# Convolution norm and swish in two pieces ahead of the recurrence's turns, block inverse by predicated copy on 128 partitions

## What is computed

```python
# conv group: GLU -> causal depthwise conv (width 31) -> LayerNorm over channels -> swish
mu = jnp.mean(of, axis=-1, keepdims=True)
var = jnp.mean(jnp.square(of - mu), axis=-1, keepdims=True)
of = (of - mu) * lax.rsqrt(var + LN_EPS) * ln_g + ln_b
conv_out = jax.nn.silu(of)
# rwkv group, per token and head
sa = jnp.einsum('bhvk,bhk->bhv', S, -kk_t)
S = S * w_t[:, :, None, :] + sa[..., None] * (kk_t * a_t)[:, :, None, :] + v_t[..., None] * k_t[:, :, None, :]
y = jnp.einsum('bhvk,bhk->bhv', S, r_t)
x = x + concat(conv_out, rwkv_out) @ w_out
```

## Time and profile before

| | us |
|---|---|
| median of 3 runs | 1161.65 |
| lowest and highest run | 1160.74, 1165.13 |
| span of the profiled execution (no other time of it is given) | 1161.0 |
| PE busy | 1105.8 (95%) |
| DVE busy | 671.7 (58%) |
| ACT busy | 364.6 (31%) |
| POOL busy | 216.2 (19%) |

### The profile page before, as it was taken

One profiled execution on the slowest core, in us unless ns is written; L12 is line 12 of the kernel. 1 busy time (PEld: TensorE's weight loads), 2 busy tenths in 40 slices (PEclk: granted clock), 3 DMA queues, 4 the chain that ended last, 5 costly groups with the idle time before them and its releaser, 6 DMA issues.

```text
span 1161.0 us, 24215 instructions
## 1 busy us (share of the span) xinstructions
PE 1105.8 (95%) x9392; PEld 668.9 (58%) x9393; DVE 671.7 (58%) x1144; ACT 364.6 (31%) x720; POOL 216.2 (19%) x278
## 2 busy tenths in 40 slices
PE   7999999999999799999999999967999999999987
PEld 5666666666666788999984555534333333333343
DVE  6388999993554788888744232365343443434416
ACT  6000011011322657777641211022223232222324
POOL 4000000010001213323320001002233342332200
PEclk9999999999998899999999999977999999999998
DMA  9211111010000111111242321057999899999739
GB/s 280 69 36 37 37 37 43 20 43 23 1 1 5 16 21 19 19 18 18 52 148 83 109 73 47 35 221 289 394 350 324 306 326 346 416 407 407 297 126 388
DMA packets 97151, 170.92 MB, mean 147 GB/s; under 512 B 44362, under 2 KB 68609, under 8 KB 87779
## 3 DMA queue, kind: packets, MB, share of 16 engines
q1 hardware_dynamic: 89571, 151.79, 36.8%
q0 software_dynamic: 7488, 17.84, 4.4%
HBM read 153.11 MB, written 25.91 MB: 154 GB/s over the span
## 4 chain that ended last, share of the span: by engine, by line
PE 82%; DVE 9%; DMA 5%; ACT 1%; issue 1%; SPq 1%; POOLq 0%; DVEq 0%; ACTq 0%
PE ps L1654 27%; PE ps L2119 14%; PE ps L1969 10%; PE ps L2149 7%; PE ps L1666 6%; PE ps L1687 3%; PE ps L2106 2%; DMA arena<-in_w_exp_up_dram 2%; PE ps L2184 2%; PE ps L1675 1%; DVE arena L2457 1%; PE ps L1999 1%; DMA arena<-in_w_exp_down_dram 1%; DVE arena L2460 1%; DVE arena L2423 1%
## 5 line engine op out<-in xcount | busy, mean ns | idle before, releaser
L1654 PE MATMUL ps<-arena 128*128 128x384 f32 (+1 forms) x1032 | 316.6, 468 | 0.0
L1654 PEld LDWEIGHTS ps<-arena 128*128 128x128 f32 x1032 | 195.3, 190 | 118.0 <-issue 1.9
L2119 PE MATMUL ps<-arena 128*64 x416 | 188.5, 596 | 3.5 <-DVE arena L2874 2.0
L2122 PE MATMUL ps<-arena 128*64 128x512 f32 x416 | 188.5, 596 | 0.0
L2271 DVE SCALAR_TENSOR_TENSOR arena<-arena,cw 128x1024 f32<-128x1024 f32 x240 | 168.2, 777 | 0.4
L2119 PEld LDWEIGHTS ps<-arena 128*64 128x64 f32 x416 | 54.4, 136 | 112.2 <-issue 112.1
L1969 PE MATMUL ps<-arena 128*128 128x512 f32 x256 | 113.1, 596 | 0.0
L1666 PE MATMUL ps<-arena 64*64 64x64 f32 x2960 | 98.2, 219 | 5.9 <-DVE arena L2471 1.7
L2149 PE MATMUL ps<-arena 128*64 x208 | 96.5, 607 | 2.4 <-ACT arena L1411 2.4
L1666 PEld LDWEIGHTS ps<-arena 64*64 64x64 f32 x2960 | 92.3, 135 | 8.6 <-issue 4.7
L2152 PE MATMUL ps<-arena 128*64 128x512 f32 x208 | 96.5, 607 | 0.0
(11 more groups left out here) (365 smaller groups left out, 1536.1 us busy)
## 6 DMA issues: line engine op xcount, KB each, us to landing
arena<-in_w_exp_gate_dram SPq DMA_DIRECT2D x32, 1024.0 KB
arena<-in_w_exp_up_dram SPq DMA_DIRECT2D x32, 1024.0 KB
arena<-in_w_exp_down_dram SPq DMA_DIRECT2D x32, 1024.0 KB, 9.8
arena<-in_w_in_dram SPq DMA_DIRECT2D x22, 512.0 KB, 4.1
arena<-in_x_prompt_dram SPq DMA_DIRECT2D x16, 512.0 KB, 8.3
arena<-y_rows SPq DMA_DIRECT2D x8, 1024.0 KB, 16.0
arena<-in_w_out_dram SPq DMA_DIRECT2D x2, 2048.0 KB
xn_rows<-arena SPq DMA_DIRECT2D x8, 512.0 KB, 2.8
```

The costliest lines, as they stand in the source:

```text
L1654: ins = pe.matmul(banks(proj_bank(q) + piece)[:, 0:n1 - n0], win[q % 6][:, c, :], xnT[:, c, n0:n1], start=(c == 0), stop=(c == DC - 1))
L2119: pe.matmul(banks(b)[0:HS, :], xgT[b][:, c, 0:HS], wring_gu[:, bass.ds(slot, 1), 0:2, c, :].rearrange("p a w f -> p (a w) f"), start=(c == ...
L2122: ins = pe.matmul(banks(b)[HS:P, :], xgT[b][:, c, HS:P], wgu[b][:, :, c, :], start=(c == 0), stop=(c == DC - 1))
```

## The change

conv_norm, conv_tanh and conv_swish no longer handle 128 tokens per turn but whole pieces: 512, 512, and the 64 sample tokens at the end as before. The root of piece 0 is taken by ACT behind conv_square(1) (j = 11), and conv_norm(0) follows on DVE behind conv_sum(3). conv_root(1), conv_tanh(0) and conv_tanh(1) stand in ACT's list behind the whole projection loop and ahead of conv_square(2); conv_norm(1) and conv_swish(0) stand in DVE's list behind scaled_a_b(0) and ahead of turn 0; conv_swish(1), and behind it the memset of x_flat, stand in turn 0 ahead of masked_k. conv_root(2) is in turn 3. The sigmoids go to conv_gate, a buffer shared by pieces 0 and 1.

PT gets its unit diagonal once (unit_diagonal, for each of the two buffers), and first_level copies the product under the mask with copy_predicated. The blocks are loaded twice, onto partitions 0 to 63 and 64 to 127, and small_blocks runs on both copies; whole_blocks joins rows 0 to 3 of the upper half on the one and rows 4 to 7 on the other half of the partitions, and a last pair of sums writes both to partitions 0 to 63.

```diff
         w_aa = at(O_EX + N, C)
-        sqt = [at(O_WIN + 8 * C, CT, C), at(O_WIN, CT, C), at(O_WIN + ZW + N + 16 + CT * C, CT, NS)]
+        sqt = [at(O_WIN + 8 * C, CT, C), at(O_WIN, CT, C), at(O_WIN + ZW + N + 16, CT, NS)]
+        conv_gate = at(O_WIN + 8 * C, CT, C)
...
-        def conv_tile(i, r):
-            return co[:, :, i * P:i * P + r]
-
-        def conv_sig(i, r):
-            return (yT[:, i + 1, :, :] if i < NT - 2 else kb)[:, :, 0:r]
+        def conv_rows(p):
+            n0, n1 = PIECES[p]
+            return co[:, :, n0:n1]
+
+        def conv_std(p):
...
-                sp.dma_start(blk, u_blocks.rearrange("g q i k -> (g q) (i k)")).then_inc(u_in, 16)
+                for copy in (slice(0, 64), slice(64, P)):
+                    sp.dma_start(blk[copy, :], u_blocks.rearrange("g q i k -> (g q) (i k)")).then_inc(u_in, 16)
                 sp.wait_ge(blk_done, 2 * j + 2)
...
+
+            def conv_root(p):
+                act.wait_ge(cvar_done, p + 1)
+                act.activation(conv_std(p), conv_std(p), ACT.Sqrt).then_inc(cstd_done, 1)
+
+            def conv_tanh(p):
+                v = conv_rows(p)
+                act.wait_ge(ln_step, p + 1)
+                g0, b0 = PR["ln_g"][0], PR["ln_b"][0]
+                for c in range(CT):
+                    ins = act.activation(v[:, c, :], v[:, c, :], ACT.Identity, scale=prm[:, g0 + c:g0 + c + 1],
+                                         bias=prm[:, b0 + c:b0 + c + 1])
+                ins.then_inc(ln_sig, 1)
+                act.wait_ge(ln_sig, 2 * p + 1)
+                act.wait_ge(ln_done, p)
+                act.activation(conv_sig(p), v, ACT.Tanh).then_inc(ln_sig, 1)
...
@@ -1159,9 +1182,13 @@
                     key_scale(0)
                 if j == 11:
                     conv_square(1)
+                    conv_root(0)
                 if j == ZT - 2:
                     exps(0)
 
+            conv_root(1)
+            conv_tanh(0)
+            conv_tanh(1)
             conv_square(2)
...
-
-            def conv_tanh(i):
-                r = tokens_of(i)
-                act.wait_ge(ln_step, 3 * i + 2)
-                act.wait_ge(ln_done, i)
-                g0, b0 = PR["ln_g"][0], PR["ln_b"][0]
-                for c in range(CT):
-                    v = co[:, c, i * P:i * P + r]
-                    ins = act.activation(v, v, ACT.Identity, scale=prm[:, g0 + c:g0 + c + 1],
-                                         bias=prm[:, b0 + c:b0 + c + 1])
-                ins.then_inc(ln_step, 1)
-                act.wait_ge(ln_step, 3 * i + 3)
-                act.activation(conv_sig(i, r), conv_tile(i, r), ACT.Tanh).then_inc(ln_sig, 1)
...
+                if j == 3:
+                    conv_root(2)
...
-                if j:
-                    conv_tanh(i)
...
-                    act.wait_ge(cvar_done, len(PIECES))
-                    for v in conv_rstd:
-                        ins = act.activation(v, v, ACT.Sqrt)
-                    ins.then_inc(cstd_done, 1)
-            conv_tanh(NT - 1)
+            conv_tanh(2)
...
+            def conv_norm(p):
+                dve.wait_ge(cstd_done, p + 1)
+                link(dve.reciprocal(conv_std(p), conv_std(p)))
+                v = conv_rows(p)
+                dve.tensor_tensor(v, v, conv_std(p).unsqueeze(1).broadcast_to(v.shape), ALU.mult).then_inc(ln_step, 1)
+
+            def conv_swish(p):
+                v = conv_rows(p)
+                dve.wait_ge(ln_sig, 2 * p + 2)
+                dve.scalar_tensor_tensor(out=v, in0=conv_sig(p), scalar=1.0, in1=v, op0=ALU.add, op1=ALU.mult)\
+                    .then_inc(ln_done, 1)
...
                     conv_eps(0)
                     conv_sum(3)
+                    conv_norm(0)
                 if j == 12:
                     conv_eps(1)
             conv(len(taps))
             link(dve.tensor_tensor(eye2, ident[:, 0:64], ident[:, 64:128], ALU.add))
-            dve.memset(x_flat, 0.0)
             scaled_a_b(0)
+            conv_norm(1)
+            conv_swish(0)
 
             def over(m, nc_):
                 return m.unsqueeze(1).unsqueeze(1).broadcast_to([P, nc_, CT, 64])
@@ -2406,8 +2430,12 @@
                 dve.wait_ge(gb_psum, j + 1)
                 if j >= 2:
                     dve.wait_ge(u_out, 16 * 2 * NB * (j - 1))
-                link(dve.tensor_tensor(pt, gb[:, :, :, 0, :], over(mask[:, 0, :], nc_), ALU.mult))
-                dve.tensor_tensor(pt, pt, over(eye2, nc_), ALU.add).then_inc(pt_done, 1)
+                dve.copy_predicated(pt, over(mask[:, 0, :].bitcast(U32), nc_), gb[:, :, :, 0, :]).then_inc(pt_done, 1)
+
+            def unit_diagonal(pt):
+                return dve.tensor_copy(pt, over(eye2, 2))
+
+            link(unit_diagonal(PT[0]))
...
             def small_blocks(j):
-                dve.wait_ge(u_in, 16 * (j + 1))
+                dve.wait_ge(u_in, 32 * (j + 1))
                 for k in range(half - 2, 0, -1):
                     n = half - 1 - k
                     tmp = blk_t.rearrange("p i j -> p (i j)")[:, 0:2 * k * n].rearrange("p (d i j) -> p d i j", d=2, i=k)
-                    link(dve.tensor_tensor(tmp, pair[:, :, 0:k, k:k + 1].broadcast_to([64, 2, k, n]),
-                                           pair[:, :, k:k + 1, k + 1:half].broadcast_to([64, 2, k, n]), ALU.mult))
+                    link(dve.tensor_tensor(tmp, pair[:, :, 0:k, k:k + 1].broadcast_to([P, 2, k, n]),
+                                           pair[:, :, k:k + 1, k + 1:half].broadcast_to([P, 2, k, n]), ALU.mult))
                     link(dve.tensor_tensor(pair[:, :, 0:k, k + 1:half], pair[:, :, 0:k, k + 1:half], tmp, ALU.add))
 
             def whole_blocks(j):
                 if j:
                     dve.wait_ge(xx_psum, level_count(j - 1, 5, 1))
-                tmp = blk_tmp.rearrange("p (i j k) -> p i j k", i=half, j=half)
-                part = blk_t.rearrange("p i j -> p (i j)")[:, 0:half * half].rearrange("p (i k) -> p i k", i=half)
+                rows = half // 2
+                tmp = blk_tmp.rearrange("p (i j k) -> p i j k", i=rows, j=half)
+                part = blk_t.rearrange("p i j -> p (i j)")[:, 0:rows * half].rearrange("p (i k) -> p i k", i=rows)
                 up = whole[:, 0:half, half:BK]
-                for n, (left, right, out) in enumerate(((whole[:, 0:half, 0:half], up, part),
-                                                        (part, whole[:, half:BK, half:BK], up))):
-                    link(dve.tensor_tensor(tmp, left.unsqueeze(2).broadcast_to([64, half, half, half]),
+                link(dve.tensor_copy(whole[64:P, 0:rows, 0:half], whole[64:P, rows:half, 0:half]))
+                for n, (left, right) in enumerate(((whole[:, 0:rows, 0:half], up), (part, whole[:, half:BK, half:BK]))):
+                    link(dve.tensor_tensor(tmp, left.unsqueeze(2).broadcast_to([P, rows, half, half]),
                                            right.rearrange("p k j -> p j k").unsqueeze(1)
-                                           .broadcast_to([64, half, half, half]), ALU.mult))
-                    ins = dve.tensor_reduce(out, tmp, AX.X, ALU.add)
+                                           .broadcast_to([P, rows, half, half]), ALU.mult))
                     if n == 0:
-                        link(ins)
-                ins.then_inc(blk_done, 1)
+                        link(dve.tensor_reduce(part, tmp, AX.X, ALU.add))
+                dve.tensor_reduce(up[0:64, 0:rows, :], tmp[0:64], AX.X, ALU.add)
+                dve.tensor_reduce(up[0:64, rows:half, :], tmp[64:P], AX.X, ALU.add).then_inc(blk_done, 1)
...
-            def conv_norm(i, s):
-                r = tokens_of(i)
-                if i == 0 and s == 0:
-                    dve.wait_ge(cstd_done, 1)
-                if s:
-                    dve.wait_ge(ln_step, 3 * i + s)
-                v = conv_tile(i, r)
-                rstd = conv_rstd[0][:, i * P:i * P + P] if r == P else conv_rstd[1]
-                if s == 0:
-                    ins = dve.reciprocal(rstd, rstd)
-                else:
-                    ins = dve.tensor_tensor(v, v, rstd.unsqueeze(1).broadcast_to([P, CT, r]), ALU.mult)
-                ins.then_inc(ln_step, 1)
-
-            def conv_swish(i):
-                r = tokens_of(i)
-                dve.wait_ge(ln_sig, i + 1)
-                v = conv_tile(i, r)
-                dve.scalar_tensor_tensor(out=v, in0=conv_sig(i, r), scalar=1.0, in1=v, op0=ALU.add, op1=ALU.mult)\
-                    .then_inc(ln_done, 1)
...
                 if j == 0:
                     conv_centre(2)
                     shifted_mix(ZT - 1, ORDER[MT - 1], z_last, zd_last)
+                    unit_diagonal(PT[1])
                 decay_add(j + 1)
...
+                    conv_swish(1)
+                    dve.wait_ge(ln_done, 2)
+                    dve.memset(x_flat, 0.0)
                 if j >= 2:
                     gn_centre(j - 2)
                 if j >= 3:
```

(45 more changed lines are left out.)

## The result

The changed kernel takes 1169.0 us (median of 13 runs), the kernel before 1164.16 in the same session (13 runs). The ratio is 1.0041, with a 95% interval from 1.0026 to 1.0055: +4.8 us, between 3.0 and 6.4. That is inside the 0.5% which the prediction took as no difference, with the interval reaching just over it; the forecast was +5.1. The forecast time, 1166.8 us, is 2.2 short, because the kernel before ran at 1164.16 here and not at the 1161.65 of its first 3 runs.

The account below looks back on a forecast made before the run. PE bounds the steady turns; at the recurrence's start, work put uncovered into DVE's queue ahead of decay_add(1) moves the end. 8.9 - 0.9 - 2.0 - 0.9 = +5.1 us on 1161.65 gives 1166.8 us, range 1157.5 to 1171.5.

Parts of the forecast that it names:

- The start: Ahead of decay_add(1): conv_norm(1), conv_tanh(0), conv_swish(0), behind ACT's late conv_root(1), delay first_level(0); decay_add(1) ends 8.9 us later.
- the copy: unit_diagonal on DVE, a copy of 512, twice before decay_add(1) is done: taken as 0.5 us, between 0.35 and 0.7.
- DVE's arm: Before conv_swish(0): DVE's division and product for conv_norm(1) done at 370.0; ACT's Identities and Tanh, at 370.8, the later.
- The rule of the Trainium skill: Each ACT table switch also drains 1.38 us: sum +7.9 us, 1169.5; dearer switches or slow predicated copy had chance 0.10.
- The clock: PE's restart after some 12 us idle: counted nothing; rivals 1 to 2 us gain (chance 0.12) or loss (0.06).
- The hidden parts: conv_norm(0), 5.4 us, in DVE's 8.28 wait; conv_swish(1) and memset in 4.47 before masked_k(0): cost nothing.
- The join in turn 0: whole_blocks on 128 partitions, on the chain in turn 0: 2.5 us instead of 3.44, so -0.9 us.
- Turns 1 to 6: DVE reaches new_state 0.9 us sooner, so PE's 0.34 us stall at chain_rhs goes each turn: -2.0 us.
- the second load: SP's second load of the blocks, 0.51 us more issue, PT 0.7 sooner: nothing, with margins of 0.5 and 0.56 us.
- signs of being wrong: first_level(0) before 370, DVE waiting for block loads, turns under 25 us, or a step behind conv_root's load over 2 us.
- the late load: Rival, chance 0.08: the two block loads hinder each other by 2 us, costing seven times 0.94 us: 1173.4.
- Turn 7: The chain goes through the blocks, DVE 0.9 us sooner, PE idle 1.43 us at 571.83: -0.9 us.

Follow-up runs that it names:

- e3: Changed kernel with conv_root(1) and conv_tanh(0) on ACT ahead of the last projected tile's copies; 1161.31 us, ratio 0.9981 to the kernel before.
- e5: e3 with the second load of the blocks issued from ACT's queue, ahead of norms_wide; 1161.22 us, ratio 0.9972 to the kernel before.
- e9: e3 once more, unchanged, to tell it from the kernel before; 1161.1 us against 1163.89, ratio 0.9961.
- e1: Kernel before with the convolution's move alone, PT and blocks as before; 1171.61 us, ratio 1.0067 to the kernel before.
- e8: e5 with y_plus_bonus moved behind scaled_r_k's first product in POOL's queue; 1167.36 us, ratio 1.0023 to the kernel before.
- e2: Kernel before with predicated copy, second load and join on 128 partitions, convolution as before; 1161.05 us, ratio 0.9983 to the kernel before.
- e4: e3 with one load of the blocks onto 128 partitions instead of two onto 64; 1171.22 us, ratio 1.0062 to the kernel before.

## Why the prediction was right

**The start, +8.9 forecast, +8.2 measured at decay_add(1) and +7.7 at gram(1).** The step that carries it holds: the root stands behind the last copies (364.60), DVE's 9.92 us of idleness can't be used, and e3 shows it by changing that order alone. The single prices: Tanh's end at 370.6, less the 1.96 (forecast 370.8); the swish 2.29 (2.4); the copy 0.42 (0.5); the predicated copy 0.73 (0.7, between 0.35 and 1.38); the four Identities 2.91 (3.1); only the reciprocal was dearer, 3.35 (3.1), and DVE's arm was not the later of the two. No drain stands behind a table load: 364.60 + 1.28 ends at 365.88 and the root starts at 365.90. The rule of the Trainium skill, "ScalarE: Activation LUTs", section "What ACT_TABLE_LOAD costs", which gave 1169.5, is not borne out by these rows, near as its figure is to the measured median.

**The clock.** I counted nothing, and nothing is the sum, of two errors of 0.7 us. Windows of the changed kernel, with the columns of the earlier trace rows:

```profile
380.00:385.20 5.20, 5.13 (x50) 4.91 (x52) 4.64 (x9) 3.98 (x9) 0.00 (x0) 0.59 0.12 28
...
400.00:409.10 9.10, 9.10 (x242) 8.92 (x242) 2.53 (x6) 5.57 (x14) 0.50 (x1) 0.92 0.19 29
```

In the kernel before the mean granted clock was 0.50 from 370 to 376, the lower level (1.2 GHz), and 1.00 from 390.33 to 398.74, the stretch that answers to the second window. So the first restart is a little quicker: gram at 382.07 takes 3.04 us where one at the lower level takes 3.68, and 0.7 is back at masked_k(0). The second is slower, 0.92 over 9.1 us, and masked_k(1) loses 0.7. That both errors are of one size is no property of the longer idleness: e3, e5 and e9 make the same exchange behind 3.19 us (gram 3.16 to 3.28 us, then 13.23 to 13.27 from gram(1) to masked_k(1)), and e1, behind 10.98 us, has the 3.68 and 12.50 of the kernel before (3.68 and 12.49). What decides between the two isn't shown.

**The hidden parts** were hidden: conv_norm(0) in DVE's wait for the next projected tile; the swish of piece 1 and the memset in front of masked_k(0), with 0.25 us left where I had "almost 1".

**The join in turn 0, forecast -0.9, measured +0.1.** This term was wrong. Timeline of DVE and POOL there:

```profile
388.71 1.26 POOL L837 TENSOR_TENSOR arena<-arena 128x512 f32<-128x512 f32 x1 [23.50 <-ACT arena L1121]
388.85 1.15 DVE L2484 COPY arena<-arena 64x32 f32<-64x32 f32 x1
```

The small copy that the join adds takes 0.18 us in a steady turn and 1.15 here: it ends at 390.00, 0.03 behind POOL's instruction (388.71 + 1.26 = 389.97). whole_blocks lasts 3.76 us in turn 0 (3.66 before) and 2.80 in a steady turn (3.44), where I had taken 2.5: 0.64 sooner, not 0.9. And small_blocks, which I took as unchanged, lasts 2.55 us on 128 partitions and 2.45 on 64, so that new_state comes 0.55 us sooner behind masked_k (7.16 in the turns on time, 7.70 before). In the kernel before, the join's products in turn 0 lay beside the same instruction of POOL, so a full gain was not to be had there. That the neighbour stretches DVE's instruction was tested by e8 for new_state's; for this copy two other traces show it. In e2 and e8 the copy comes just ahead of POOL's instruction and takes 0.18 us, and the product behind it takes 1.53 and 1.69 us instead of 0.59.

**Turns 1 to 6, forecast -2.0, measured -1.6.** The size fits; its making doesn't. I had 0.34 us per turn as "the most there is", from the turn at 458.83. That was the smaller of the stalls. A turn earlier the kernel before shows, timeline of PE:

```profile
430.75 2.03 PE L1666 MATMUL ps<-arena 64*64 64x64 f32 x64
433.09 1.15 PE L1666 MATMUL ps<-arena 64*64 64x64 f32 x32 [0.31 <-DVE arena L2471]
434.17 1.16 PE L1625 MATMUL ps<-small,arena 64*128 64x128 f32 x16
```

From 430.75 to 434.17 are 3.42 us; the same stretch of the changed kernel, free of the stall, takes 2.90 (415.37 to 418.27). That is the whole gain of turn 1, whose period is 25.21 instead of 25.74. From turn 3 on PE comes to this place 0.15 us later, in both kernels, because of the finished tile that it turns first. So the stall was 0.38 us there (3.28 before, 2.90 in e8), near my 0.34, and 0.52 only in turns 1 and 2.

Two things took part of it back. POOL's y_plus_bonus stretches new_state in the later turns on time: 3.06 us instead of 2.90 (491.74 to 494.80), the collision that e8 removes. And the second load, which I costed at nothing with a margin of 0.5 and 0.56 us, was late twice, one of the signs of being wrong that I had named. The stores did start 0.69 us sooner (7.83 us ahead of masked_k and not 7.14), but in the turn at 459.54 they took longer to land, and the loads were issued only 0.21 sooner than in that turn before. DVE was released 3.78 us behind the first of them, where one load had been in time with 2.83. New_state came 0.57 and 0.33 us later than in the turns on time. The two periods are 25.79 and 25.54, against 25.51 on time: in these turns new_state's second instruction starts when POOL is all but through and takes 0.43, so lateness is in part paid for by the collision that it avoids. The six changes of period are -0.53, -0.50, +0.05, -0.24, -0.20 and -0.15, in sum -1.6. So the late load, the rival at 0.08, is real, but cost 0.3 us in all beside the turns on time (0.6 if these were free of POOL's stretch) where I had 6.6.

**Turn 7, -0.9 forecast, -0.7 measured**, as the saving of the join is shorter (0.64). **Elsewhere**, -1.0 us comes from the stages behind, which the change doesn't touch. No run here tells why, and it is the difference of two single executions.

So the step that carries the forecast, the order in ACT's queue, is right and shown, and the sum hit partly by luck, in cancelling: the join fell short by 1.0 in turn 0 and by 0.6 behind it, against a start cheaper by 0.7 and the 1.0 from elsewhere.

## What to carry to other kernels

Work moved into an engine's idle time is free only if what it reads is ready by then: look up where its producer stands in the other engine's queue, and move the producer with it. Here one reordering on ACT turns +4.8 us into -2.2 (e3) and -4.5 (e9, the same kernel again), so that the change beats both kernels; e5 (0.9972) does it too, and nothing shows that its other queue adds to that. When a step gets shorter by half a microsecond, read again what reaches it from the side, the transfer and the neighbour, and read the stall in more than one turn before calling it the most there is.

## What the runs showed of the hardware

- DVE beside POOL: a two-input instruction of 256 elements took up to 1.46 us where it takes 0.42 alone, the longer the sooner behind POOL's it began: 0.74 in the turn at 450.33 of e5, 1.45 in both kernels where it starts 0.10 us behind POOL's (before, 465.18 and 465.08). It ended 0.27 to 0.29 us behind POOL's, and went back to 0.42 when POOL's was moved (e8). By the Trainium skill, "SBUF — State Buffer", section "SBUF: two separate sides", an instruction of DVE with two SBUF inputs and one of GpSimd that reads SBUF take turns at a port pair, each for its whole length. The ends in these traces agree with that. A copy of 64x32 took 1.15 instead of 0.18; it has one input, and for it only the rows speak.
- One 128 KB load onto 128 partitions released its reader 4.93 us behind its issue (e4); two loads of 64 KB did it 3.78 us behind the first, in a late turn. The same page of the Trainium skill, section "Can I just issue two DMAs to hit both halves?", says that only one transfer over all 128 partitions reaches every port, which speaks for the single load. For this load, whose source is read twice, the measurement decides for two.
- The reciprocal took 0.541 us at 64 elements, 0.911 at 128 and 3.35 at 512: 5.8 ns for each element more, then 6.3. A predicated copy of 512 elements from PSUM takes 0.735 us, a masking 0.692.
- The length of PE's idleness did not decide what its restart cost. The first gram behind it took 3.04 us behind 11.06 us of idleness (the changed kernel), 3.68 behind 10.98 (e1), 3.68 behind 2.85 (before), 3.28 behind 3.19 (e3), and 3.68 behind 6.89 us at 395.92; at full clock it takes 1.92.
